# Keys turned in 32-element squares by VectorE and DMA, input sums spread over four blocks of the down product, on one Trainium2 core

## The reference, cut to what matters

```python
u = rms_norm(h, g_mix_pre[i])
qa, ka, va, qb, kb, vb = split_projection(u, w_in[i])
if cache is None:
    oa = mixer_a_prompt(qa, ka, va, rel_bias[i])
    ob = mixer_b_prompt(qb, kb, vb, lam, lam0, diff_subln[i])
    new = (ka[:, h.shape[1] - keep:], va[:, h.shape[1] - keep:], kb, vb)
else:
    oa = mixer_a_sample(qa, ka, va, ca_k, ca_v, past, rel_bias[i])
    ob = diff_attention(qb, jnp.concatenate([cb_k, kb], axis=1), jnp.concatenate([cb_v, vb], axis=1), ...)
    new = (ka, va, kb, vb)
g_a, g_b = jnp.split(jax.nn.sigmoid(u @ w_gate[i]), 2, axis=-1)
mix = (g_a * (oa @ w_branch_a[i]) + g_b * (ob @ w_branch_b[i])) @ w_out[i]
h = h + rms_norm(mix, g_mix_post[i])
f = jnp.square(jax.nn.relu(rms_norm(h, g_ffn_pre[i]) @ w_up[i])) @ w_down[i]
h = h + rms_norm(f, g_ffn_post[i])
h = h + jax.nn.sigmoid(h @ w_ple_gate[i]) * rms_norm(ple @ w_ple[i], g_ple[i])
```

## Time and profile before

| | |
|---|---|
| median of the runs | 1146.62 us |
| profiled execution, time | 1147.33 us |
| profiled execution, span | 1145.7 us |
| TensorE busy | 1107.4 us, 97% |
| VectorE busy | 578.8 us, 51% |
| ScalarE (ACT) busy | 514.7 us, 45% |
| GpSimd (POOL) busy | 533.7 us, 47% |
| DMA | 99.15 MB, mean 87 GB/s |

### The profile page before, as it was taken

How to read it: one execution, slowest core, us unless ns; L and a number is a source line. 1 busy time by engine, 2 the same in 40 slices (tenths; PEclk the granted TensorE clock), 3 DMA queues, 4 the chain that set the end, 5 groups by cost and what they waited for, 6 DMA issues and landing times.

```text
span 1145.7 us, 23097 instructions
## 1 busy us (share of the span) xinstructions
PE 1107.4 (97%) x8360; PEld 1063.3 (93%) x8360; DVE 578.8 (51%) x1200; ACT 514.7 (45%) x1115; POOL 533.7 (47%) x456
## 2 busy tenths in 40 slices
PE   9799999999999999999999999789999999999998
PEld 7799999999889889999999989789999999999897
DVE  5566656656655541112432657866515712732755
ACT  6255555555555553231233463325614632552552
POOL 3456655565554433334445544334444434354551
PEclk9899999999999999999999999999999999999999
DMA  7233432333323322232222212213322232232123
GB/s 181 65 95 88 126 89 76 94 104 87 95 86 96 95 68 82 80 100 81 82 83 82 66 47 83 75 55 93 101 83 85 83 98 82 77 102 83 56 74 84
DMA packets 167394, 99.15 MB, mean 87 GB/s; under 512 B 8833, under 2 KB 162682, under 8 KB 167314
## 3 DMA queue, kind: packets, MB, share of 16 engines
q1 hardware_dynamic: 159570, 82.05, 25.0%
q0 software_dynamic: 7744, 16.02, 4.6%
HBM read 88.57 MB, written 11.02 MB: 87 GB/s over the span
## 4 chain that ended last, share of the span: by engine, by line
PE 63%; issue 19%; POOL 9%; DVE 5%; ACT 2%; DMA 1%; POOLq 0%; SPq 0%; ACTq 0%; DVEq 0%
PE proj L1711 45%; POOL w_lo L537 9%; PE score L1834 3%; PE proj L2030 2%; PE turn_out L1901 2%; PE turn_out L1931 2%; PE turn_out L1923 1%; PE turn_out L1870 1%; PE proj L2117 1%; PE turn_out L1928 1%; PE score L1845 1%; PE proj L1991 1%; PE proj L1791 1%; DMA x_tm<-x_prompt 1%; DVE sq_sum L1405 1%
## 5 line engine op out<-in xcount | busy, mean ns | idle before, releaser
L537 POOL TENSOR_TENSOR w_lo<-w_raw,w_hi 128x512 fp32r<-128x512 f32 x292 | 387.2, 1333 | 495.7 <-ACT w_hi L725 495.0
L725 ACT ACTIVATE w_hi<-w_raw 128x512 fp32r<-128x512 f32 x292 | 180.9, 628 | 297.5 <-PE proj L1711 266.2
L1711 PE MATMUL proj<-act_hi,w_hi 128*128 128x288 f32 x1088 | 247.0, 309 | 0.8 <-ACT wide L968 0.3
L1711 PE MATMUL proj<-act_lo,w_hi 128*128 128x288 f32 x1088 | 233.7, 297 | 0.0
L1711 PE MATMUL proj<-act_hi,w_lo 128*128 128x288 f32 x1088 | 233.3, 296 | 0.0
L1711 PEld LDWEIGHTS proj<-act_hi,w_hi 128*128 128x128 f32 x1088 | 172.6, 190 | 12.5 <-issue 7.8
L1711 PEld LDWEIGHTS proj<-act_lo,w_hi 128*128 128x128 f32 x1088 | 175.6, 189 | 0.0
L1711 PEld LDWEIGHTS proj<-act_hi,w_lo 128*128 128x128 f32 x1088 | 175.5, 189 | 0.0
L1711 PE MATMUL proj<-mid_hi,w_hi 128*128 128x288 f32 x608 | 131.7, 298 | 12.0 <-DVE wide L1536 9.8
L1711 PE MATMUL proj<-mid_hi,w_lo 128*128 128x288 f32 x608 | 131.0, 297 | 0.0
L1711 PE MATMUL proj<-mid_lo,w_hi 128*128 128x288 f32 x608 | 130.9, 296 | 0.0
(11 more groups left out here) (322 smaller groups left out, 2139.6 us busy)
## 6 DMA issues: line engine op xcount, KB each, us to landing
w_raw<-w_in SPq DMA_DIRECT2D x72, 256.0 KB, 2.9
w_raw<-w_up SPq DMA_DIRECT2D x64, 256.0 KB, 2.8
w_raw<-w_down SPq DMA_DIRECT2D x64, 256.0 KB, 2.8
w_raw<-w_gate SPq DMA_DIRECT2D x32, 256.0 KB, 2.7
w_raw<-w_branch_b SPq DMA_DIRECT2D x16, 256.0 KB, 2.8
w_raw<-w_out SPq DMA_DIRECT2D x16, 256.0 KB, 2.8
w_raw<-w_ple_gate SPq DMA_DIRECT2D x16, 256.0 KB, 2.8
out<-k_tm POOLq DMA_DIRECT2D x12, 256.0 KB, 2.8
```

The lines of the kernel that those rows point to most:

```text
L537: pool.tensor_tensor(w_lo[:, slot], w_raw[:, slot], w_hi[:, slot].bitcast(F32), ALU.subtract).then_inc(lo_done, 1)
L725: act.activation(w_hi[:, slot], w_raw[:, slot], ACT.Copy).then_inc(hi_done, 1)
L1711: last = pe.matmul(out[:, h], w[:, slot, at], x[:, k, HALF * h:HALF * h + HALF], start=(k == 0 and s == 0), stop=(k == blocks - 1 and s == 2))
```

## The change

Keys no longer go through TensorE to be turned.

- **Keys' outputs.** VectorE turns each unit's keys `kT` (128 features x 576 tokens) in squares of 32 x 32 into `k_out` (step K4). The squares are put in their places by DMA: for each of the four groups of 32 partitions one DMA for the prompt's 512 tokens and one for the sample's 64, in runs of 32 floats (128 bytes). These eight DMAs are issued by SP (`keys_of`), after a wait for `k_turned`.
- **Cached keys.** Four DMAs of SP load them in runs of 128 bytes, with the squares already in the places of the turned matrix; VectorE turns the squares (`ckT`, step CK). ACT rounds `ckT` to `ckT_hi`, POOL subtracts to `ckT_lo`. TensorE's sample scores wait for `ck_split`.
- TensorE loses K4, CK and the keys' part of Tail; ACT the copy to `k_tm`; VectorE the subtraction for `ckT_lo` and the copy of the sample's keys; POOL the load of `ck` and two of four output DMAs of a unit.
- SP's loops over the units are written out; the first six pieces of the gate's weights are issued by the same function. `keys_of(u-2)` stands behind the third piece of unit u.
- **Input sums.** In the down product of group 0 the four sums are made in blocks 0, 2, 3 and 5 (`X_SUMS_AT`) in place of 0, 1, 2 and 3. ACT splits them between the two weight pieces of the block. A k-step waits for its own block of `up_split`, not for the pair's.
- **Up pairs.** On VectorE `up_low` of the `up_t` half moves behind `make_sums`, and `sum_low(pair + 1, 0)` behind line 1629.

```diff
-        if name in ("V4", "K4", "T", "OT", "Tail", "CK"):
+        if name in ("V4", "T", "OT", "Tail"):
...
-    A_TURNS, B_TURNS = 14, 11
+    A_TURNS, B_TURNS = 12, 9
+    SQ = 32
...
+        X_SUMS_AT = (0, 2, 3, 5)
...
+            def squares(rows_, col, a):
+
+                return rows_[:, col + SQ * a:col + SQ * a + SQ].rearrange("(c t) f -> t c f", t=SQ)
+
+            def square_rows(x, a, first, last):
+
+                return x[SQ * a:SQ * a + SQ, first:last].rearrange("t (c f) -> t c f", f=SQ)
+
+            def load_ck(eng, u):
+                c, col = (cbk, P * u) if u < NB else (cak, P * (u - NB))
+                for a in range(P // SQ):
+                    eng.dma_start(square_rows(ck, a, 0, SEQ), squares(c, col, a)).then_inc(ck_loaded, 16)
+
+            def keys_of(u):
+
+                outs, col = (out_b, P * u) if u < NB else (out_a, P * (u - NB))
+                sp.wait_ge(k_turned, u + 1)
+                for a in range(P // SQ):
+                    sp.dma_start(squares(outs[0], col, a), square_rows(k_out, a, 0, SEQ)).then_inc(k_stored, 16)
+                    sp.dma_start(squares(outs[2], col, a), square_rows(k_out, a, SEQ, T)).then_inc(k_stored, 16)
+                if u + 1 < NU:
+                    sp.wait_ge(ck_turned, u + 1)
+                    load_ck(sp, u + 1)
...
+                        piece(Count(u * 6 + 2 * n + kh), src)
+                        if n == 1 and kh == 0 and u >= 2:
+                            keys_of(u - 2)
...
+                    elif name == "CK":
+
+                        at_least(pool, ck_hi, u + 1)
+                        pool.tensor_tensor(ckT_lo[:, :], ckT[:, :], ckT_hi[:, :].bitcast(F32), ALU.subtract
+                                           ).then_inc(ck_split, 1)
...
-                        act.activation(ckT_hi[:, :], turn[:, 0:SEQ], ACT.Copy).then_inc(ck_hi, 1)
+                        at_least(act, ck_turned, u + 1)
+                        act.activation(ckT_hi[:, :], ckT[:, :], ACT.Copy).then_inc(ck_hi, 1)
...
+            for j in range(KB - 2):
+                down_piece(Count(0), 2 * j)
+                if j in X_SUMS_AT:
+                    split_x_sums(X_SUMS_AT.index(j))
+                down_piece(Count(0), 2 * j + 1)
...
+                        at_least(dve, ck_loaded, (u + 1) * 64)
+                        at_least(dve, ck_split, u)
+                        dve.transpose(ckT[:, :], ck[:, :]).then_inc(ck_turned, 1)
+                    elif name == "K4":
+                        at_least(dve, kq_split, u * 2 + 2)
+                        at_least(dve, k_stored, u * 128)
+                        dve.transpose(k_out[:, :], kT[par][:, :]).then_inc(k_turned, 1)
...
-                    if q:
-                        up_low(group, up_t, 2 * q - 2, 2 * q)
                     sum_low(pair, 2)
...
                     if q < PAIRS - 1:
                         make_sums(pair + 1, p + RING)
+                    if q:
+                        up_low(group, up_t, 2 * q - 2, 2 * q)
...
+                    if q:
+                        at_least(dve, up_split, group * KB + 2 * q)
                     dve.tensor_tensor(up_t[:, HALF:T], bank_c, u_two[:, :], ALU.subtract).then_inc(u_made, 1)
+                    at_least(dve, w_used, p + 3)
+                    dve.tensor_tensor(up_t[:, 0:HALF], bank_a, p1_kept[:, :], ALU.add).then_inc(c11_ready, 1)
                     if q < PAIRS - 1:
                         sum_low(pair + 1, 0)
-                    at_least(dve, w_used, p + 3)
-                    dve.tensor_tensor(up_t[:, 0:HALF], bank_a, p1_kept[:, :], ALU.add).then_inc(c11_ready, 1)
...
-                if 0 < j <= KB // 2:
-                    x_sums_low(j - 1)
-                if j < KB // 2:
-                    make_x_sums(j)
+                if j - 1 in X_SUMS_AT:
+                    x_sums_low(X_SUMS_AT.index(j - 1))
+                if j in X_SUMS_AT:
+                    make_x_sums(X_SUMS_AT.index(j))
...
+                    at_least(pe, ck_split, u + 1)
...
-                        for j in range(QB - 1):
-                            last = pe.transpose(turn[:, P * j:P * j + P], ck[:, P * j:P * j + P], ident[:, :])
...
-                        last = pe.transpose(turn[0:SMP, P:2 * P], kT[par][:, SEQ:T], ident[:, :])
...
-                            input_ready=lambda k: at_least(pe, up_split, group * KB + (k // 2 * 2 + 2)))
+                            input_ready=lambda k: at_least(pe, up_split, group * KB + (k // 2 * 2 + 2 if group.const else k + 1)))
```

More of the change, by code:

```diff
@@ L338, in encoder_layer @@
         tab_ready = sem("tab_ready")
-        ck_loaded, cv_loaded, kv_stored = sem("ck_loaded"), sem("cv_loaded"), sem("kv_stored")
+        ck_loaded, cv_loaded, k_stored, v_stored = (sem(n) for n in ("ck_loaded", "cv_loaded", "k_stored", "v_stored"))
+        k_turned, ck_turned, ck_split = sem("k_turned"), sem("ck_turned"), sem("ck_split")
         scored, biased, exped, combined = sem("scored"), sem("biased"), sem("exped"), sem("combined")
@@ L440, in two_tasks, with unit_pieces @@
                         piece(Count(p0 + 2 * kh + j), k_half(w, kh, cols[j]))
-            def unit_pieces(u0, u, cols):
-                for n, base in enumerate(cols):
-                    for kh in range(2):
-                        piece(u * 6 + (2 * n + kh), k_half(w_in[0], kh, ((u + (-u0)) * P + base).value()))
+            def squares(rows_, col, a):
[15 more added lines that the diff above has]
+                    load_ck(sp, u + 1)
+            def unit_pieces(u):
+                for n in range(3):
+                    for kh in range(2):
+                        if u < NB:
+                            src = k_half(w_in[0], kh, P * u + b_cols[n])
+                        elif u < NU:
+                            src = k_half(w_in[0], kh, P * (u - NB) + a_cols[n])
+                        else:
+                            src = k_half(w_gate[0], kh, P * (3 * (u - NU) + n))
+                        piece(Count(u * 6 + 2 * n + kh), src)
+                        if n == 1 and kh == 0 and u >= 2:
+                            keys_of(u - 2)
             for g, at in ((g_mix_post, 8), (g_ffn_pre, 16), (g_ffn_post, 24), (g_ple, 32)):
@@ L456, in _, with stage @@
             sp.dma_start(band_row, band_sb[:, :]).then_inc(band_row_kept, 16)
-            with sp.Fori(0, (NB - 2) // 2) as it:
-                for v in range(2):
-                    unit_pieces(0, Count(1 + v, [(it, 2)]), b_cols)
-            unit_pieces(0, Count(NB - 1), b_cols)
-            with sp.Fori(0, NA // 2) as it:
-                for v in range(2):
-                    unit_pieces(NB, Count(NB + v, [(it, 2)]), a_cols)
-            def stage(p0, w, n, kblocks=4, halves_=2):
+            for u in range(1, NU + 2):
+                unit_pieces(u)
+            def stage(p0, w, n, kblocks=4, halves_=2, first=0):
                 per = RING // halves_
@@ L1064, in split_x_sums @@
                     act.activation(t[:, k], t_raw[:, i], ACT.Copy).then_inc(xs_hi, 1)
-            for j in range(KB):
-                if j < KB - 2:
-                    for i in range(2):
-                        down_piece(Count(0), 2 * j + i)
-                if j < KB // 2:
-                    split_x_sums(j)
+            for j in range(KB - 2):
[3 more added lines that the diff above has]
+                down_piece(Count(0), 2 * j + 1)
             last_pieces(Count(1))
@@ L1186, in projected @@
                 dst = (kT[par], q_raw, vT)[n][:, :]
+                if n == 0 and not gates:
+                    at_least(dve, k_turned, u + (-1))
                 if n == 1 and not gates:
@@ L1265, in unit @@
                     elif name == "CK":
-                        at_least(dve, ck_hi, u + 1)
-                        dve.tensor_tensor(ckT_lo[:, :], turn[:, 0:SEQ], ckT_hi[:, :].bitcast(F32), ALU.subtract
-                                          ).then_inc(turn_free, 1)
+                        at_least(dve, ck_loaded, (u + 1) * 64)
[5 more added lines that the diff above has]
+                        dve.transpose(k_out[:, :], kT[par][:, :]).then_inc(k_turned, 1)
                     elif name == "S":
@@ L1275, in unit @@
                         at_least(dve, turned, turns + (t + 1))
[L1276 removed]
                         if prev != "B":
[L1278 removed]
+                            dve.tensor_copy(v_tm[0:SMP, QB - 1], turn[0:SMP, 0:P]).then_inc(turn_free, 1)
                         else:
[L1280 removed]
+                            dve.tensor_copy(v_tm[0:SMP, QB - 1], turn[0:SMP, 0:P]).then_inc(tail_copied, 1)
                             at_least(dve, o_hi, u * 2)
```

56 lines of the change are left out of this document (20 added, 36 removed).

## The result

The changed kernel took 1137.67 us (median of four runs, 1137.39 to 1138.13), the kernel before in the same runs 1146.59 us: ratio 0.9927, 95% interval 0.9912 to 0.9942. That is 8.9 us faster. Forecast were 20.0 us and 1126.6 us, with a range from 1121 to 1136: the sign was right, and more than half of the gain didn't come. The profiled execution took 1138.13 us with a span of 1136.6 us (1145.7 before), at a granted clock of 0.990 of full speed.

A forecast was written before the change was run, and what follows sets the result against it. TensorE, busy 97% of the span, was taken to bound the kernel. Terms: 11.9 (transposes) - 2.0 (B units) + 8.1 (down product) + 2.0 (up pairs) = 20.0 us, so 1146.6 - 20.0 = 1126.6 us; range 1121 to 1136.

The forecast's parts named there:

- Transposes off TensorE: Attention: TensorE loses CK, K4 and the keys' part of Tail, 0.99 us a unit, 11.9 us for twelve units.
- VectorE's transposes: Attention, steps CK and K4: VectorE's transposes take 0.7 and 0.76 us, with 1.8 us as upper end beside POOL.
- The loss in B units: Attention: TensorE waits anew after K4 on VectorE's busy stretch, 0.25 us a B unit, 2.0 us for eight.
- A units leave microseconds between N and T, so nothing there: Attention, A units: slack between two steps of the unit covers K4 on VectorE, so no loss is counted.
- DMA and SP: Attention: 128-byte runs at 28.7 ns a packet and SP's twelve issues a unit are covered; cost nothing.
- Down product: Group 0: sums in blocks 0, 2, 3, 5 and the finer wait cut lost time to 4.9 us; gain 8.1 us.
- 1.05 us more for each POOL `w_lo`: Down product of group 0: VectorE's low parts cost 2.6 us, plus 1.05 us per `w_lo` beside them.
- Up pairs: Up pairs: TensorE's waits for line 1629, 2.0 us in three groups, go; gain 2.0 us.
- With `up_low` behind `make_sums` that wait is covered: Up pairs: VectorE's 1.5 us wait for ACT's square of the `up_t` half is covered by 2.8 us of sums.
- next is line 1629 itself: Up pairs: the next limit is 5.2 us of VectorE's work after the third product, where TensorE has 6.4 us.
- (a): Attention: VectorE's chain replaces the transposes in B units, which lose 7 us in place of 2.0: 1131.6 us; chance 0.10.
- (b): Down product: the loop only moves, 9 us lost in place of 4.9, 1 more in first pair: 1131.7 us; chance 0.08.

The follow-up runs named there:

- e11_pool_calm: Changed kernel with POOL's `ckT_lo` behind `k_lo` in A units only and its four band-table DMA issues spread one a unit: 1132.3 us, ratio 0.9873.
- e8_no_lo: Changed kernel with POOL's `w_lo` cut to two columns for twelve weight pieces of group 0's down product (low parts old values): 1128.3 us, ratio 0.9834.
- e10_split_early: Changed kernel with finer waits at the input sums: ACT splits earlier, each low part waits for its own high part only: 1131.3 us, ratio 0.9866.
- e1_up_old: Changed kernel with VectorE's order in the up pairs as before the change: 1138.7 us, ratio 0.9933.

## Why the prediction was off

- **Transposes off TensorE, 11.9 us.** Right. Undisturbed units win 0.9 to 1.0 us, for 0.99 predicted.
- **VectorE's transposes, 0.7 and 0.76 us.** Right, and the upper bound of 1.8 us beside POOL is refuted. Duration of the twelve on line 1300 (min, median, max in ns), then one of them and the `w_lo` that ran beside it:

```profile
L1300 DVE STREAM_TRANSPOSE k_out<-kT x12: 761/769/772, 58.3 to 407.6; 128x576 f32<-128x576 f32 x12
```

```profile
182.22 0.77 DVE L1300 STREAM_TRANSPOSE k_out<-kT 128x576 f32<-128x576 f32 x1
```

```profile
182.25 1.29 POOL L570 TENSOR_TENSOR w_lo<-w_raw,w_hi 128x512 fp32r<-128x512 f32 x1 [1.45 <-ACT w_hi L753]
```

  The transpose isn't held at all; seven of the twelve ran beside a `w_lo`. The rule of the Trainium skill that the prediction weighed (SBUF — State Buffer, SBUF: two separate sides: only operations with two SBUF inputs, or in a 2-port mode, compete with GpSimd) agrees with this.
- **The loss in B units, 0.25 us each.** It was sought at K4 and C2, and units 7 and 8 lose nothing. The step that failed is the sentence on POOL: "POOL gets the 1.3 us subtraction and loses three DMA issues of some 0.8 us; it waits for ACT most of the time." It counts POOL's time, where its order was the matter. In the third unit the subtraction holds VectorE where the issue it replaced did not; it lengthens POOL's runs without a gap; and it stands ahead of `o_r`. The third unit and A units, whose POOL queues differ from the B unit that I read, were not looked at: "A units leave microseconds between N and T, so nothing there." Together 5.4 us: in `e11_pool_calm` the third unit, the interval into the first A unit and the third A unit are 2.7, 1.6 and 1.1 us shorter than in the changed kernel.
- **DMA and SP, nothing.** Right, and dearer than need be. The keys' outputs moved from POOL's queue q0 to SP's q1, so both count: 31.8% x 16 x 1136.6 us after, and 29.6% x 16 x 1145.7 before (q1 in the earlier trace rows, 25.0%, and 4.6% of q0), are 5783 and 5426 us. The 52224 packets more, for the same bytes, cost 6.8 ns each and not 28.7 ns; the DMA share of a B unit is 0.36, not 0.49. That the Trainium skill (DMA: Bandwidth & Descriptors, Specifications) sets 512 bytes as the least for line rate doesn't show in the time at this load.
- **Down product, 8.1 us: 6.2.** The mechanism was right (waits at blocks 5 and 6, and a late first pair), the term for collisions too small: "1.05 us more for each POOL `w_lo`", right in itself, was counted once or twice a sum where four ran in a row (6.9 us of low parts, from 720.1 to 727.0 us, in place of some 3.7). Forecast were no wait at block 3, 2.1 us at block 5 and 1.2 at block 6; measured 0.47, 1.39 and 2.25. After the last one TensorE went on below full clock (first pair of matmuls 0.81 us, as at 744.95 us in the earlier trace rows), where I had forecast full; the stretch of it (PE, PEld, DVE, ACT, POOL, PEclk, DMA share, GB/s):

```profile
748.00:754.00 6.00, 3.75 (x20) 3.52 (x19) 5.93 (x8) 0.00 (x0) 2.40 (x2) 0.80 0.47 136
```

- **Up pairs, 2.0 us: -1.3.** The step that failed is "With `up_low` behind `make_sums` that wait is covered". It was, but the loop then ran through the weight slots, whose load, at 892.29 us, ended just where POOL's next `w_lo` began; its length was 12.2 us, as good as before (12.05). "next is line 1629 itself" named a chain of 5.2 us and left out what it starts from. The loss of 1.1 us in group 1 is the late first pair, as `e8_no_lo` (34.0 us) and `e10_split_early` (34.4) show. What the order alone is worth isn't shown: `e1_up_old` stays within what traces of the changed kernel's feed-forward code vary by.
- **Rivals.** (a), VectorE's chain, happened in a form that was not described: the time that it gave up was POOL's to take. (b) was half right for the down product: its loss, with the first pair of group 1, moved rather than went.

What stays open: the units 4 to 6 win 0.3 us less than 7 and 8, in `e11_pool_calm` too, and the interval into the first A unit takes 36.2 us, hardly less than before; TensorE still waits 1.6 us for `o_tm` there. For that, `o_r` would have to go ahead of a `w_lo` that waits for ACT. This was not tried.

## What to carry to other kernels

Where VectorE and POOL both work on SBUF, an operation has a place as well as a length: list POOL's operations without a gap, lay VectorE's operations on SBUF over them, those with two inputs first, and read this for each kind of unit, not for the typical one. An edit that frees 1 us of TensorE may be paid back by an innocent 1.3 us on POOL; moved again, it lands on something else, so look at what VectorE does in the idle stretch that you move it to. When one limit of a loop is lifted, write down the next loop in full, through the buffers and their loads, before counting the gain.

## What the runs showed of the hardware

- Beside POOL, VectorE can be held for more than one of POOL's operations: 3.92 us for an operation of 0.35 us beside three of POOL in a row, 2.67 for 0.48, both to the end of POOL's run. It isn't always the whole run: the operation on one column at 116.75 us ended at 117.99 us, with `ckT_lo`, as POOL's next operation began. What decides between the two isn't shown.
- A DMA issue by POOL holds some of VectorE's operations. From 109.36 to 113.67 us, beside four issues, all had their normal length. But a CAST of 64 x 64, 0.19 us elsewhere, took 0.50 us in the changed kernel beside an issue and nothing else of POOL, and ended with it:

```profile
326.26 0.50 DVE L1227 CAST q_pad_hi<-q_hi 64x64 fp32r<-64x64 f32 x1
```

```profile
325.96 0.82 POOL L632 DMA_DIRECT2D out<-v_tm  x1 [0.30 <-DVE mid_lo L1369]
```

  Another, at 168.24 us, took 2.30 us, through two issues and the `w_lo` behind them. The 24 CASTs into `q_pad_hi` took 18.5 us in place of 8.7, the largest single part of VectorE's 22.9 us more. They cost no time that these runs show: units 7 and 8, with CASTs of 1.94 and 2.29 us, win the full 1.0 us.
- The operation held for 3.92 us has one tensor in SBUF as input and a scalar of one column for each partition, and the CAST has one input. So one input alone doesn't make an operation safe; the transpose, with one input too, was not held. By the Trainium skill (SBUF — State Buffer, SBUF: two separate sides) an operation in a 2-port mode competes with GpSimd too, which would tell them apart; no run here shows in which mode any of them ran.
- A transpose of fp32 in 32 x 32 squares on VectorE takes what a plain operation of that size takes: 0.70 us for 128 x 512, 0.77 for 128 x 576.
- Cutting 512-byte runs into runs of 128 cost the DMA engines 6.8 ns for each packet added, cutting those into 64 bytes 6.7 ns (from shares rounded to 0.1%): at the same bytes, a packet more is cheap here.
